# Values projected with the tokens standing, in a two-layer hybrid retention kernel

## The chip, the cores and the metric

The kernel runs as one program on one core of a Trainium2 chip. The metric is the device time of one execution in microseconds (us). Inputs lie in the chip's memory when it starts, and the output is written there.

## The reference, cut to what matters

A backbone of two layers over 512 latent tokens and 256 context tokens of width 1024, in float32. Each layer has a modulated RMS norm, one input projection whose columns feed three token mixers, an output projection, a second norm and a gated MLP with a convolution over tokens.

```python
q = _heads(p[..., Q0:K0], B, T)                          # p = h @ w_in, 512 columns each for q, k, v
k = _heads(p[..., K0:V0], B, T) * RET_HEAD_DIM ** -0.5
v = _heads(p[..., V0:G0], B, T)
q, k = apply_rope(q, cos, sin), apply_rope(k, cos, sin)  # latent tokens only
scores = jnp.einsum('bnihd,bnjhd->bnhij', qc, kc) * intra
o_intra = jnp.einsum('bnhij,bnjhe->bnihe', scores, vc)   # vc: values by chunk of 128 tokens
u = jnp.einsum('bnjhd,hj,bnjhe->bnhde', kc, zeta, vc)    # chunk states
o_cross = jnp.einsum('bnihd,hi,nbhde->bnihe', qc, xi, prev)
```

Keys, values and queries have 8 heads of 64. Both sums over j run over tokens, so TensorE wants values, and the keys of the states, with tokens on the partitions. Modulation vectors for later norms (`mods`) are dot products of columns of `w_mod` with silu(c).

## The kernel before, in words

**Layout.** Activations stand with features on the 128 partitions and tokens along the row: `h_hi`, `h_lo` are [128, 8 blocks, 768 tokens], the latent tokens first (0 to 511), then the context (512 to 767). Every number is split into a high part in the matmul's format and a rest, and each product is three matmuls: w_hi x_hi, w_lo x_hi, w_hi x_lo.

**Slabs.** All weights come as one stream of 206 slabs of 128 x 1024 numbers (512 KB), in the order of `stream_plan`. SP loads slab s into `raw[s % 2]` once slab s-2 is split (its wait on `split`); GpSimd splits each half into `w_hi[s % 2]` and `w_lo[s % 2]` (`split_half`, L475 and L477) once TensorE has finished the same half of slab s-2; TensorE multiplies (`tile`, L1316: one row block, three products, each over the column ranges `cols`) into the PSUM buffer `pair[s % 2]`, and ScalarE or VectorE copies it out and counts in `drained[s % 2]`. TensorE's `begin` waits for the first half's split and for the copy of slab s-2.

**The projection before.** Slabs 0 to 7 of a layer alternate one key block (128 features) and one value block, all 768 tokens; slabs 8 to 11 are the query blocks (layer 1: latent tokens only). Slabs 0 and 1 are interleaved with the norm that feeds them. ScalarE copies keys to `kT` and values to `Y` with features on the partitions. After each key and query slab, `swap` sends four DMAs from ScalarE's queue that copy the block with its 32-row quarters exchanged into `rot`, and VectorE's `rope` (L1007 to L1009) combines the two. During query slab 1 (the second), TensorE also transposes the values: after each of the first six row blocks, four 128x128 transposes for one chunk of 128 tokens (L1578) into one of two PSUM banks, which ScalarE copies to `vtok` (L674). During query slab 3 it does the same for the keys, into `ktok` (L680).

**Other work in this stretch.** ScalarE, in program order of layer 0 (L657 to L682): copy key 0, swap, copy value 0, Silu of `c_b` (L665), copy key 1, swap, copy value 1, wait for VectorE's L814 and Exp (L668), copy key 2, swap, copy value 2, the decay tables (`decays`, 28 small Exps, L515 to L526), copy key 3, swap, copy value 3, and then the value chunks and the queries. In layer 1 `decays` stands after value 0. VectorE, in order of layer 0: for each key j, rope and then `ring_mods` of 3, 3, 2, 2 modulation columns (`MODS_KVQ`; a column is two dot products over 1024, L790, and an addition, L793, which counts `mod_used`); after key 1's columns comes `log_decays` (L813 to L825), whose second instruction, L814, frees ScalarE's Exp. The dot products also write a scratch of 1024 columns in PSUM (`aux01`). The columns come through two slots: SP issues a slot's load only when `mod_used` shows it free, in one queue with the slab loads, so that here a slab's load stands behind a wait for VectorE (L392 to L403).

**After the projection**, the first mixer slabs (`mixer_plan`) run between the steps of retention, which VectorE paces with the masks and scaled values (`vz` from `vtok`, `St`, `qxi`).

```python
                act.wait_ge(s["decay_ready"], 1)
                for c in range(NLC + NCC):
                    act.wait_ge(s["tr_done"], c + 1)
                    nc.scalar.activation(vtok[:, c, :], aux(2 + c % 2), ACT.Copy).then_inc(s["v_moved"], 1)
```

Of the kernel before, what the change touches and what calls it, by code (L numbers as in the profile page):

```python
# [18 lines left out]
P = 128  # L19
T, C = 512, 256  # L20
# [36 lines left out]
def stream_plan():  # L57

    at, plan = 0, {}
    for l in range(DEPTH):  # L60
        for name, n in (("kv", 2 * HB), ("q", HB), ("cch", 2 * FB), ("cbf", 2 * FB), ("g", HB),
                        ("dft", dft_slabs(l)), ("out", KB)):
            plan[l, name] = at
            at += n
        for g, n in enumerate(GROUPS):
            plan[l, "up", g] = at
            at += 2 * n
            plan[l, "down", g] = at
            at += KB
    plan["end"] = at  # L70
    return plan


PLAN = stream_plan()


# [44 lines left out]
MODS_OUT = 2  # L121
MODS_UP = 2
MIXER_LEAD = KB
MIXER_TAIL = 4
# [53 lines left out]
def build_program(nc, io):  # L178
# [6 lines left out]
    def at(name, shape, offset, dt=fp32):  # L185
        return nc.alloc_sbuf_tensor_at(name, shape, dt, offset=offset)
# [46 lines left out]
    vtok = at("vtok", [P, NLC + NCC, 4 * P], work + 49152)  # L233
    z = at("z", [P, FB, TC], work + 61440)
    state = at("state", [P, NLC + 1, H, HD], work + 67584)
    St = at("St", [P, 2, 4, CH], work + 79872)
# [109 lines left out]
    with block:  # L346

        @block.sync
        def _(sp):
# [67 lines left out]
            for g, n in enumerate(GROUPS):  # L417
# [21 lines left out]
            s = PLAN[1, "kv"]  # L439
            load_slabs(s, 1)  # L440
# [15 lines left out]
        def _(pool):  # L456
# [30 lines left out]

            behind = {PLAN[0, "up", 0] + 2: "n2_0", PLAN[1, "kv"] + 2: "n1_1", PLAN[1, "up", 0] + 2: "n2_1"}
            for s in range(PLAN["end"]):
# [6 lines left out]
        def _(act):  # L496
# [135 lines left out]
            for l in range(DEPTH):  # L632
# [23 lines left out]

                kv, q0 = PLAN[l, "kv"], PLAN[l, "q"]  # L657
                for j in range(HB):
                    copy_out(kv + 2 * j, kT[:, j, :], TC)
                    swap(kT[:, j, 0:T], kv + 2 * j, j)  # L660
                    copy_out(kv + 2 * j + 1, Y[:, j, :], TC)
                    if j == 0:
                        if l == 0:
                            act.wait_ge(c_loaded, 32)
                            nc.scalar.activation(c_b[:, :, :], c_b[:, :, :], ACT.Silu).then_inc(c_ready, 1)  # L665
                    if l == 0 and j == 1:
                        act.wait_ge(ld_ready, 1)
                        nc.scalar.activation(ldt[:, 0, :], ldt[:, 1, :], ACT.Exp, scale=-1.0).then_inc(ld_ready, 1)  # L668
                    if j == (0 if l else 2):
                        decays(l)  # L670
                act.wait_ge(s["decay_ready"], 1)
                for c in range(NLC + NCC):
                    act.wait_ge(s["tr_done"], c + 1)
                    nc.scalar.activation(vtok[:, c, :], aux(2 + c % 2), ACT.Copy).then_inc(s["v_moved"], 1)  # L674
                for j in range(HB):
                    if j == HB - 1:
                        for c in range(NLC + NCC):
                            u = NLC + NCC + c
                            act.wait_ge(s["tr_done"], u + 1)
                            nc.scalar.activation(ktok[:, c, :], aux(2 + u % 2), ACT.Copy).then_inc(s["k_moved"], 1)  # L680
                    copy_out(q0 + j, Y[:, j, 0:nlat], nlat)
                    swap(Y[:, j, 0:T], q0 + j, HB + j)  # L682

                def gate(j):
# [93 lines left out]
        def _(dve):  # L778
# [7 lines left out]

            def mod_dots(slab, col, acc, used):

                for st in range(2):
                    chain(nc.vector.tensor_tensor_reduce(out=aux01[:, :], in0=slab, in1=c_b[:, st, :], scale=1.0,  # L790
                                                         scalar=0.0, op0=ALU.mult, op1=ALU.add,
                                                         accum_out=mod_acc[:, acc, st:st + 1]), mod_dots.base)
# [5 lines left out]
            def ring_mods(m, n):  # L798
                for j in range(m, m + n):
                    dve.wait_ge(mod_loaded[j % 2], 16 * (j // 2 + 1))  # L800
                    mod_dots(mod_slot[j % 2][:, :], MOD_START + j, j % 2, mod_used)

# [193 lines left out]
            for l in range(DEPTH):  # L996
# [14 lines left out]
                for j in range(HB):  # L1011
                    if j == 0:
                        dve.wait_ge(consts_loaded, 16 * 4)
                    rope(kT[:, j, 0:T], j)
                    if l == 0:
                        if j == 0:
                            dve.wait_ge(c_ready, 2)
                        ring_mods(m, MODS_KVQ[j])
                        m += MODS_KVQ[j]
                    elif j < 2:  # L1020
                        ring_mods(m, MODS_LAST)
                        m += MODS_LAST

                    if l == 0 and j == 1:
                        log_decays()
                    if j == (0 if l else 2):
                        decays(l)
                    if l and j == 1:
                        dve.wait_ge(mod_used, m)
                for j in range(HB):  # L1030
                    if l == 0 and j % 2:
                        ring_mods(m, MODS_KVQ[HB + j // 2])
# [275 lines left out]
        def _(pe):  # L1308
# [207 lines left out]
            for l in range(DEPTH):  # L1516
# [16 lines left out]
                def parts_ready(hi_sem, lo_sem, per):  # L1533

                    return lambda n: ((hi_sem, per * (n + 1)), (lo_sem, per * (n + 1)))

                kv_rest = (all_k, h_hi, h_lo, both, parts_ready(n1["hi_ready"], n1["h_ready"], 2))
                if l == 0:
# [14 lines left out]
                else:  # L1553
                    pair_behind_norm(PLAN[l, "kv"], "n1_1")
                slabs(PLAN[l, "kv"] + 2, HB - 1, all_k, h_hi, h_lo, both, None)

                n = 0
                for j in range(HB):
                    q = PLAN[l, "q"] + j
                    if j == 1:  # L1560
                        pe.wait_ge(*drained_by(PLAN[l, "kv"] + 2 * HB - 1))
                        pe.wait_ge(n1["nt_ready"], 2 * KB)
                    elif j == 3:
                        pe.wait_ge(s["roped"], HB)
                    begin(j % 2, q, pair_uses(q - j % 2))
                    for k in range(KB):
                        tile(j % 2, q, k, all_k, h_hi, h_lo, cols, None)
                        if j % 2 == 0 or k >= NLC + NCC:
                            continue
                        if n >= 2:  # L1570
                            last = n - 2
                            if last < NLC + NCC:
                                pe.wait_ge(s["v_moved"], last + 1)
                            else:
                                pe.wait_ge(s["k_moved"], last - (NLC + NCC) + 1)
                        src = Y if j == 1 else kT
                        for b in range(HB):
                            ins = nc.tensor.transpose(aux(2 + n % 2)[:, b * P:b * P + P], src[:, b, k * CH:k * CH + CH],  # L1578
                                                      ident[:, :])
                        ins.then_inc(s["tr_done"], 1)  # L1580
                        n += 1


                n_state = n_chunk = 0
# [25 lines left out]
                for item in mixer_plan(l):  # L1610
# [242 lines left out]
```

## Time and profile before

| | us |
|---|---|
| three runs, median | 1607.3 |
| lowest, highest | 1603.33, 1608.1 |
| the profiled execution's own time | 1607.85 |
| its span | 1606.1 |

| engine | busy us | share of the span | instructions |
|---|---|---|---|
| TensorE, matmuls (PE) | 1547.5 | 96% | 8910 |
| TensorE, weight loads (PEld) | 1296.8 | 81% | 8910 |
| VectorE (DVE) | 933.3 | 58% | 1331 |
| ScalarE (ACT) | 340.9 | 21% | 529 |
| GpSimd (POOL) | 900.5 | 56% | 841 |

The mean granted clock of TensorE was 0.987 of full speed. Matmuls are pipelined: they overlap in the profile, so the distance between two starts tells what one costs in a stream, and its duration does not. Weight loads lie beside the matmuls. An idle time in brackets is that of the engine before the instruction, with what ended it. DMA issues stand under the queue of the engine that sends them (ACTq, SPq). Layer 0's input projection lies between about 26 and 147 us, layer 1's between about 960 and 1059 us.

### The profile page before, as it was taken

Reading aid. Unit: us, or ns where it says so; the run is one execution under the profiler, and the core shown is the slowest. Engines: PE = TensorE matmul, PEld = TensorE weight load, DVE = VectorE, ACT = ScalarE, POOL = GpSimd, SP = SyncE. Lnnn points to the kernel's source line nnn. Section 1 sums busy time; section 2 is a strip of 40 time slices with the busy share of each in tenths; the row PEclk is TensorE's granted clock in tenths of the full one; section 3 lists DMA queues with packets and bytes.
Section 4 is the critical chain, followed back from the end, with each engine's and each line's share of the span. In section 5 each row is a group of like instructions: output and inputs, shape, how many; then the busy total and the mean of one; then the engine's idle time right before and its main releaser. Section 6 shows DMA issues by size and latency. Waiting matters only on the chain.

```text
span 1606.1 us, 24230 instructions
## 1 busy us (share of the span) xinstructions
PE 1547.5 (96%) x8910; PEld 1296.8 (81%) x8910; DVE 933.3 (58%) x1331; ACT 340.9 (21%) x529; POOL 900.5 (56%) x841
## 2 busy tenths in 40 slices
PE   7999989999999999999999999998999999999997
PEld 5888778886888888888888878876777888888886
DVE  4695556697788847882488547366555441341434
ACT  4332112313211101120012224111323220220221
POOL 2364233656555645554555446563475777777773
PEclk9999999999999999999999999999999999999999
DMA  9344111343333333332333222231122322223222
GB/s 377 133 144 132 40 33 47 129 159 117 108 114 131 131 130 119 118 118 65 118 118 127 83 91 93 79 105 53 53 92 66 100 96 92 97 99 106 95 92 100
DMA packets 50080, 172.70 MB, mean 108 GB/s; under 512 B 6240, under 2 KB 8800, under 8 KB 48992
## 3 DMA queue, kind: packets, MB, share of 16 engines
q1 hardware_dynamic: 46080, 165.70, 30.5%
q10 hardware_dynamic: 3936, 6.14, 1.3%
q8 instruction: 41, 0.67, 0.2%
q14 instruction: 23, 0.19, 0.0%
HBM read 165.52 MB, written 2.10 MB: 104 GB/s over the span
## 4 chain that ended last, share of the span: by engine, by line
PE 84%; DVE 9%; DMA 2%; POOL 2%; ACT 1%; issue 1%; SPq 0%; ACTq 0%; DVEq 0%; POOLq 0%
PE pair L1316 76%; PE pair L1425 3%; DVE qxi L1130 2%; DVE h_lo L939 1%; DVE nt L933 1%; DMA start_slot<-in_start_mods 1%; POOL w_lo L477 1%; PE aux L1662 1%; DMA raw<-in_slabs 1%; PE aux L1668 1%; PE aux L1578 1%; PE aux L1626 1%; DVE St L1134 1%; DVE aux L790 1%; POOL w_hi L475 1%
## 5 line engine op out<-in xcount | busy, mean ns | idle before, releaser
L475 POOL TENSOR_SCALAR w_hi<-raw 128x512 fp32r<-128x512 f32 (+1 forms) x410 | 300.4, 733 | 634.6 <-PE pair L1316 523.1
L477 POOL TENSOR_TENSOR w_lo<-raw,w_hi 128x512 fp32r<-128x512 f32 (+1 forms) x410 | 585.5, 1428 | 34.3
L1316 PE MATMUL pair<-h_hi,w_hi 128*128 128x512 f32 x1760 | 531.2, 360 | 6.8 <-DVE tv L1254 2.2
L1316 PE MATMUL pair<-h_lo,w_hi 128*128 128x512 f32 x1760 | 527.2, 357 | 2.7 <-DVE h_lo L1156 2.6
L1316 PE MATMUL pair<-h_hi,w_lo 128*128 128x512 f32 x1760 | 523.9, 355 | 0.0
L1316 PEld LDWEIGHTS pair<-h_hi,w_hi 128*128 128x128 f32 x1760 | 289.2, 189 | 64.6 <-issue 6.9
L1316 PEld LDWEIGHTS pair<-h_lo,w_hi 128*128 128x128 f32 x1760 | 289.3, 189 | 53.5 <-DVE h_lo L1156 4.2
L1316 PEld LDWEIGHTS pair<-h_hi,w_lo 128*128 128x128 f32 x1760 | 287.7, 189 | 47.5
L790 DVE CUSTOM_DVE_ANT_0 aux<-mod_slot,c_b 128x1024 f32<-128x1024 f32 x160 | 223.9, 1399 | 4.3 <-DMA mod_slot<-in_mods 1.1
L1209 DVE SCALAR_TENSOR_TENSOR x<-pair,modv,x 128x256 f32 (+3 forms) x84 | 53.0, 658 | 173.2 <-PE pair L1316 173.0
L1316 PE MATMUL pair<-hid_lo,w_hi 128*128 128x512 f32 x486 | 147.7, 358 | 0.0
L1316 PE MATMUL pair<-hid_hi,w_hi 128*128 128x512 f32 x486 | 147.3, 357 | 0.0
L1316 PE MATMUL pair<-hid_hi,w_lo 128*128 128x512 f32 x486 | 146.5, 356 | 0.0
L1254 DVE SCALAR_TENSOR_TENSOR tg<-pair,vecs,tg 128x511 f32<-128x511 f32 (+1 forms) x132 | 87.1, 660 | 84.9 <-ACT tg L763 76.8
L1254 DVE SCALAR_TENSOR_TENSOR tv<-pair,vecs,tv 128x511 f32<-128x511 f32 (+1 forms) x132 | 87.2, 661 | 81.2 <-ACT tv L760 73.0
L1316 PEld LDWEIGHTS pair<-hid_hi,w_hi 128*128 128x128 f32 x486 | 80.2, 188 | 14.8
L1316 PEld LDWEIGHTS pair<-hid_hi,w_lo 128*128 128x128 f32 x486 | 80.0, 187 | 14.8
L760 ACT ACTIVATE tv<-pair,vecs 128x768 f32<-128x768 f32 (+1 forms) x44 | 35.0, 796 | 266.4 <-PE pair L1316 208.6
L1316 PEld LDWEIGHTS pair<-hid_lo,w_hi 128*128 128x128 f32 x486 | 80.6, 188 | 13.6
L763 ACT ACTIVATE tg<-pair,vecs 128x768 f32<-128x768 f32 (+1 forms) x44 | 35.0, 795 | 193.1 <-PE pair L1316 190.3
L1282 DVE TENSOR_TENSOR hid_lo<-tv,hid_hi 128x768 f32 (+1 forms) x44 | 47.1, 1070 | 44.7 <-ACT hid_hi L768 44.7
L1425 PE MATMUL pair<-h_lo,w_hi 128*128 128x256 f32 (+1 forms) x160 | 53.6, 335 | 7.8 <-DVE h_lo L939 6.1
(171 smaller groups left out, 1294.7 us busy)
## 6 DMA issues: line engine op xcount, KB each, us to landing
raw<-in_slabs SPq DMA_DIRECT2D x206, 512.0 KB, 3.5
mod_slot<-in_mods SPq DMA_DIRECT2D x80, 512.0 KB, 3.5
start_slot<-in_start_mods SPq DMA_DIRECT2D x8, 1024.0 KB, 15.6
x<-in_x SPq DMA_DIRECT2D x4, 768.0 KB, 10.1
rot<-kT ACTq DMA_DIRECT2D x32, 64.0 KB, 3.3
rot<-Y ACTq DMA_DIRECT2D x32, 64.0 KB, 2.1
out<-fin SPq DMA_DIRECT2D x16, 128.0 KB, 1.9
c_b<-in_c SPq DMA_DIRECT2D x1, 512.0 KB, 7.6
```

Of the source, the lines that this page charges most:

```text
L475: nc.gpsimd.tensor_scalar(w_hi[p][:, a:b], raw[p][:, a:b], 1.0, 1.0, ALU.mult, ALU.mult).then_inc(split, 1)
L477: nc.gpsimd.tensor_tensor(w_lo[p][:, a:b], raw[p][:, a:b], w_hi[p][:, a:b].bitcast(fp32), ALU.subtract).then_inc(split, 3 if narrow(s) else 1)
L760: nc.scalar.activation(tv[:, 0:nlat], pair[0][:, 0:nlat], ACT.Copy, scale=vec_dyn("ffnw", w))\
L763: nc.scalar.activation(tg[:, 0:nlat], pair[1][:, 0:nlat], ACT.Copy, scale=vec_dyn("ffnw", w + 3 * NHB)).then_inc(s["tg_ready"], 1)
L790: chain(nc.vector.tensor_tensor_reduce(out=aux01[:, :], in0=slab, in1=c_b[:, st, :], scale=1.0, scalar=0.0, op0=ALU.mult, op1=ALU.add, acc ...
L933: nc.vector.scalar_tensor_tensor(nt[k % 2][:, a:b], aux(2 + part)[:, 0:b - a], mod(l, st, sc, k), x[:, k, a:b], ALU.mult, ALU.mult).then_i ...
L1130: nc.vector.tensor_tensor(qxi[to, hh, :, :], q[r], xi[r, d, :, :], ALU.mult)\
L1209: nc.vector.scalar_tensor_tensor(x[:, 2 * i + p, a0:a1], pair[p][:, a0:a1], modv[:, st, bass.ds(2 * i + (c0 + p), 1)], x[:, 2 * i + p, a0: ...
L1254: ins = nc.vector.scalar_tensor_tensor(dst, src, vec_dyn("ffnw", w + tap), dst, ALU.mult, ALU.add)
L1282: nc.vector.tensor_tensor(hid_lo[:, i, 0:nlat], tv[:, 0:nlat], hid_hi[:, i, 0:nlat].bitcast(fp32), ALU.subtract)\
L1316: ins = nc.tensor.matmul(out[:, a:b], wt, xt[:, a:b], start=first and k == 0, stop=last and k == 2)
L1425: ins = nc.tensor.matmul(pair[p][:, a:b], wt[p][:, w], xt[:, k, a:b], start=opens and j == 0, stop=n == len(order) - 1 and j == 2, skip_gr ...
```

## The change

Values are computed with the tokens on the partitions at once: the stationary operand is a 128x128 tile of `h_hi` or `h_lo`, the moving one 512 value columns of the weights. A value slab now holds two feature blocks (k = 2j and 2j+1) of all 512 value columns. TensorE runs, for each of the two blocks and each of six token chunks, three matmuls of 512 columns, and all four value slabs accumulate in six PSUM banks: the two of `pair[1]` and the four of `aux`. After the last, ScalarE copies the six banks to `vtok`. The transposes of values and the copies of values to `Y` are gone.

The twelve slabs come in a new order: keys in 0, 1, 2, 4, values in 3, 5, 7, 9, queries in 6, 8, 10, 11. Keys are transposed in the last two query slabs: four chunks in the second half of slab 10, two at the start of slab 11, and the banks go around all four of `aux`. ScalarE's two early steps stand after key slab 1 (Silu of `c_b`, then the wait for L814 and Exp), and in layer 1 `decays` stands there too. The scratch of the dot products in this stretch is `spare`, in SBUF. VectorE's first `vz` waits for the value copies, and TensorE's wait on `mod_used` before the first scores goes.

```diff
-        for name, n in (("kv", 2 * HB), ("q", HB), ("cch", 2 * FB), ("cbf", 2 * FB), ("g", HB),
+        for name, n in (("kvq", 3 * HB), ("cch", 2 * FB), ("cbf", 2 * FB), ("g", HB),
...
+K_SLABS, V_SLABS, Q_SLABS = [0, 1, 2, 4], [3, 5, 7, 9], [6, 8, 10, 11]
+def k_slab(l, j):
+    return PLAN[l, "kvq"] + K_SLABS[j]
...
+KEYS_EARLY = 4
...
+    spare = at("spare", [P, D], work + 12288)
...
+    def v_bank(c):
+        return pair[1][:, c * 4 * P:(c + 1) * 4 * P] if c < 2 else aux(c - 2)
+    V_ORDER = [0, 1, 4, 5, 2, 3]
+    def key_bank(c):
+        return aux((c + 2) % 4)
...
+                def move_values():
+                    act.wait_ge(s["decay_ready"], 1)
+                    act.wait_ge(done, v_slab(l, HB - 1) + 1)
+                    for n, c in enumerate(V_ORDER):
+                        ins = nc.scalar.activation(vtok[:, c, :], v_bank(c), ACT.Copy)
+                        if n == 1:
+                            ins.then_inc(drained[1], HB)
+                        else:
+                            ins.then_inc(s["v_moved"], 1)
+                def move_keys(first, last):
+                    for c in range(first, last):
+                        act.wait_ge(s["tr_done"], c + 1)
+                        nc.scalar.activation(ktok[:, c, :], key_bank(c), ACT.Copy).then_inc(s["k_moved"], 1)
...
                 for j in range(HB):
-                    copy_out(kv + 2 * j, kT[:, j, :], TC)
-                    swap(kT[:, j, 0:T], kv + 2 * j, j)
-                    copy_out(kv + 2 * j + 1, Y[:, j, :], TC)
-                    if j == 0:
-                        if l == 0:
-                            act.wait_ge(c_loaded, 32)
-                            nc.scalar.activation(c_b[:, :, :], c_b[:, :, :], ACT.Silu).then_inc(c_ready, 1)
+                    copy_out(k_slab(l, j), kT[:, j, :], TC)
+                    swap(kT[:, j, 0:T], k_slab(l, j), j)
                     if l == 0 and j == 1:
+                        act.wait_ge(c_loaded, 32)
+                        nc.scalar.activation(c_b[:, :, :], c_b[:, :, :], ACT.Silu).then_inc(c_ready, 1)
                         act.wait_ge(ld_ready, 1)
                         nc.scalar.activation(ldt[:, 0, :], ldt[:, 1, :], ACT.Exp, scale=-1.0).then_inc(ld_ready, 1)
-                    if j == (0 if l else 2):
+                    if j == (1 if l else 2):
                         decays(l)
...
                 for j in range(HB):
-                    if j == HB - 1:
...
+                    if j == 2:
+                        move_values()
+                        move_keys(0, KEYS_EARLY)
+                    elif j == 3:
+                        move_keys(KEYS_EARLY, NLC + NCC)
+                    copy_out(q_slab(l, j), Y[:, j, 0:nlat], nlat)
+                    swap(Y[:, j, 0:T], q_slab(l, j), HB + j)
...
-                        ring_mods(m, MODS_KVQ[j])
+                        ring_mods(m, MODS_KVQ[j], spare)
...
+                dve.wait_ge(s["v_moved"], NLC + NCC - 1)
                 scaled_values(0)
...
+                def values(j):
+                    slab_ = v_slab(l, j)
+                    pe.wait_ge(split, 4 * slab_ + 2)
+                    if j == 0:
+                        pe.wait_ge(*drained_by(k_slab(l, 1)))
                         pe.wait_ge(n1["nt_ready"], 2 * KB)
+                    for half in range(2):
+                        if half:
+                            pe.wait_ge(split, 4 * slab_ + 4)
+                        k, w = 2 * j + half, slice(half * 4 * P, (half + 1) * 4 * P)
+                        for c in range(NLC + NCC):
+                            t = slice(c * P, c * P + P)
+                            for n, (xt, wt) in enumerate(((h_hi, w_hi), (h_hi, w_lo), (h_lo, w_hi))):
+                                ins = nc.tensor.matmul(v_bank(c), xt[:, k, t], wt[1][:, w], start=k == 0 and n == 0,
+                                                       stop=k == KB - 1 and n == 2)
+                        ins.then_inc(done if half else half_done[1], 1)
+                def turn_keys(c):
+                    if c < 4:
+                        pe.wait_ge(s["v_moved"], c + 2)
+                    else:
+                        pe.wait_ge(s["k_moved"], c - 3)
...
+                for n in range(2, 3 * HB):
+                    if n in V_SLABS:
+                        values(V_SLABS.index(n))
+                        continue
+                    p, sl = n % 2, k0 + n
+                    uses = both if n in K_SLABS else cols
+                    begin(p, sl, pair_uses(sl - p))
+                    if n == Q_SLABS[2]:
                         pe.wait_ge(s["roped"], HB)
...
+                        if n == Q_SLABS[2] and k >= KB - KEYS_EARLY:
+                            turn_keys(k - (KB - KEYS_EARLY))
+                        elif n == Q_SLABS[3] and k < NLC + NCC - KEYS_EARLY:
+                            turn_keys(KEYS_EARLY + k)
...
-                            if l == 0:
-                                pe.wait_ge(mod_used, sum(MODS_KVQ))
```

## Rows read from the trace of the kernel before

**Rows 1.** The page's chain that ended last, shares of the span by engine.
```profile
PE 84%; DVE 9%; DMA 2%; POOL 2%; ACT 1%; issue 1%; SPq 0%; ACTq 0%; DVEq 0%; POOLq 0%
```

**Rows 2.** Chain in order of time, layer 0's projection; start us, us, what.
```profile
50.78 66.34 PE pair L1316 x374
```

**Rows 3.** TensorE's timeline, layer 1; start us, us, instruction xcount [idle before <-releaser].
```profile
979.03 0.51 PE L1316 MATMUL pair<-h_hi,w_hi 128*128 128x512 f32 x2
...
1029.91 0.40 PE L1316 MATMUL pair<-h_hi,w_hi 128*128 128x512 f32 x1
...
1036.07 0.60 PE L1578 MATMUL aux<-ident_small,Y 128*128 128x128 f32 x4
...
1037.19 0.60 PE L1578 MATMUL aux<-ident_small,Y 128*128 128x128 f32 x4
...
1054.00 0.66 PE L1578 MATMUL aux<-ident_small,kT 128*128 128x128 f32 x4 [1.75 <-ACT ktok L680]
```

**Rows 4.** ScalarE's timeline, layer 0's projection.
```profile
58.12 0.81 ACT L645 ACTIVATE Y<-pair 128x768 f32<-128x768 f32 x1 [3.74 <-issue]
...
60.24 1.92 ACT L665 ACTIVATE c_b<-c_b 128x2048 f32<-128x2048 f32 x1
65.22 0.81 ACT L645 ACTIVATE kT<-pair 128x768 f32<-128x768 f32 x1 [3.06 <-PE pair L1316]
66.06 2.44 ACTq L655 DMA_DIRECT2D rot<-kT  x4
73.70 0.81 ACT L645 ACTIVATE Y<-pair 128x768 f32<-128x768 f32 x1 [7.67 <-PE pair L1316]
...
88.77 0.24 ACT L668 ACTIVATE ldt<-ldt 128x48 f32<-128x48 f32 x1 [12.96 <-DVE ldt L814]
88.92 0.79 ACT L645 ACTIVATE kT<-pair 128x768 f32<-128x768 f32 x1
...
105.43 0.81 ACT L645 ACTIVATE kT<-pair 128x768 f32<-128x768 f32 x1
```

**Rows 5.** Line L1578, TensorE's transposes: duration ns min/median/max, first and last start.
```profile
L1578 PE MATMUL aux<-ident_small,Y x48: 270/272/273, 117.0 to 1042.0; 128*128 128x128 f32 x48
```

**Rows 6.** VectorE's timeline, the same stretch.
```profile
64.84 0.16 DVE L793 TENSOR_TENSOR modv<-mod_acc,vecs 128x2 f32<-128x2 f32 x1
...
68.85 1.23 DVE L790 CUSTOM_DVE_ANT_0 aux<-mod_slot,c_b 128x1024 f32<-128x1024 f32 x1 [1.11 <-DMA mod_slot<-in_mods]
...
73.00 0.80 DVE L1007 TENSOR_TENSOR rot<-rot,rope_sin 128x512 f32<-128x512 f32 x1 [1.12 <-DMA rot<-kT]
...
76.44 1.22 DVE L790 CUSTOM_DVE_ANT_0 aux<-mod_slot,c_b 128x1024 f32<-128x1024 f32 x1
...
88.03 0.18 DVE L813 TENSOR_SCALAR ldt<-vecs 128x48 f32<-128x48 f32 x1
```

**Rows 7.** SP's timeline, the same stretch: DMA issues.
```profile
65.03 0.33 SPq L365 DMA_DIRECT2D mod_slot<-in_mods  x1
65.40 0.43 SPq L351 DMA_DIRECT2D raw<-in_slabs  x1
```

**Rows 8.** GpSimd's timeline, the same stretch.
```profile
71.96 1.29 POOL L477 TENSOR_TENSOR w_lo<-raw,w_hi 128x512 fp32r<-128x512 f32 x1
```

**Rows 9.** Windows in retention: us; PE, PEld, DVE, ACT, POOL busy (x); PEclk; DMA; GB/s.
```profile
174.00:177.00 3.00, 0.52 (x7) 0.55 (x9) 2.27 (x4) 0.00 (x0) 0.00 (x0) 0.95 0.00 0
177.00:180.00 3.00, 3.00 (x29) 2.46 (x25) 0.00 (x0) 0.00 (x0) 0.00 (x0) 0.50 0.00 0
...
183.00:186.00 3.00, 3.00 (x22) 2.27 (x21) 0.00 (x0) 1.93 (x2) 1.81 (x2) 0.92 0.00 0
```

**Rows 10.** ScalarE's timeline, layer 1, its decays.
```profile
982.27 1.28 ACT L515 ACT_TABLE_LOAD   x1
...
991.00 0.42 ACT L526 ACTIVATE cdec<-ld 64x8 f32<-64x8 f32 x2
```

**Rows 11.** Waits of TensorE; us in total, times, longest us.
```profile
PE aux L1662 <- DVE St L1134: 17.2, 7, 6.2
```

More of the change, by code:

```diff
@@ L74, with v_slab, q_slab @@
 PLAN = stream_plan()
+K_SLABS, V_SLABS, Q_SLABS = [0, 1, 2, 4], [3, 5, 7, 9], [6, 8, 10, 11]
+def k_slab(l, j):
+    return PLAN[l, "kvq"] + K_SLABS[j]
+def v_slab(l, j):
+    return PLAN[l, "kvq"] + V_SLABS[j]
+def q_slab(l, j):
+    return PLAN[l, "kvq"] + Q_SLABS[j]
 def slab_blocks(s):
@@ L438, in _ @@
                     load_slabs(PLAN[0, "down", g] + 2 + 2 * i, 1)
-            s = PLAN[1, "kv"]
+            s = PLAN[1, "kvq"]
             load_slabs(s, 1)
@@ L486, in lows @@
                         .then_inc(pool_low, 1)
-            behind = {PLAN[0, "up", 0] + 2: "n2_0", PLAN[1, "kv"] + 2: "n1_1", PLAN[1, "up", 0] + 2: "n2_1"}
+            behind = {PLAN[0, "up", 0] + 2: "n2_0", PLAN[1, "kvq"] + 2: "n1_1", PLAN[1, "up", 0] + 2: "n2_1"}
             for s in range(PLAN["end"]):
@@ L667, in _ @@
                         act.wait_ge(ld_ready, 1)
                         nc.scalar.activation(ldt[:, 0, :], ldt[:, 1, :], ACT.Exp, scale=-1.0).then_inc(ld_ready, 1)
-                    if j == (0 if l else 2):
+                    if j == (1 if l else 2):
                         decays(l)
[L671 to L674, printed above, removed]
@@ L675, in _ @@
                 for j in range(HB):
-                    if j == HB - 1:
[L677 to L682, printed above, removed]
+                    if j == 2:
[3 more added lines that the diff above has]
+                        move_keys(KEYS_EARLY, NLC + NCC)
@@ L785, in chain, with mod_dots @@
                 dve.wait_ge(dve_chain, steps[0] if base is None else base + steps[0])
-            def mod_dots(slab, col, acc, used):
+            def mod_dots(slab, col, acc, used, scratch=aux01):
                 for st in range(2):
-                    chain(nc.vector.tensor_tensor_reduce(out=aux01[:, :], in0=slab, in1=c_b[:, st, :], scale=1.0,
+                    chain(nc.vector.tensor_tensor_reduce(out=scratch[:, :], in0=slab, in1=c_b[:, st, :], scale=1.0,
                                                          scalar=0.0, op0=ALU.mult, op1=ALU.add,
@@ L796, in _, with ring_mods @@
             mod_dots.base = None
-            def ring_mods(m, n):
+            def ring_mods(m, n, scratch=aux01):
                 for j in range(m, m + n):
                     dve.wait_ge(mod_loaded[j % 2], 16 * (j // 2 + 1))
-                    mod_dots(mod_slot[j % 2][:, :], MOD_START + j, j % 2, mod_used)
+                    mod_dots(mod_slot[j % 2][:, :], MOD_START + j, j % 2, mod_used, scratch)
             def one_plus(l, kind, ready):
@@ L1017, in _ @@
                             dve.wait_ge(c_ready, 2)
-                        ring_mods(m, MODS_KVQ[j])
+                        ring_mods(m, MODS_KVQ[j], spare)
                         m += MODS_KVQ[j]
                     elif j < 2:
-                        ring_mods(m, MODS_LAST)
+                        ring_mods(m, MODS_LAST, spare)
                         m += MODS_LAST
@@ L1031, in _ @@
                     if l == 0 and j % 2:
-                        ring_mods(m, MODS_KVQ[HB + j // 2])
+                        ring_mods(m, MODS_KVQ[HB + j // 2], spare)
                         m += MODS_KVQ[HB + j // 2]
@@ L1535, in parts_ready @@
                     return lambda n: ((hi_sem, per * (n + 1)), (lo_sem, per * (n + 1)))
+                k0 = PLAN[l, "kvq"]
                 kv_rest = (all_k, h_hi, h_lo, both, parts_ready(n1["hi_ready"], n1["h_ready"], 2))
@@ L1553, in _ @@
                 else:
[L1554 to L1561, printed above, removed]
-                        pe.wait_ge(n1["nt_ready"], 2 * KB)
-                    elif j == 3:
+                    pair_behind_norm(k0, "n1_1")
@@ new lines, in turn_keys @@
+                def turn_keys(c):
[3 more added lines that the diff above has]
+                        pe.wait_ge(s["k_moved"], c - 3)
+                    for b in range(HB):
+                        ins = nc.tensor.transpose(key_bank(c)[:, b * P:b * P + P], kT[:, b, c * CH:c * CH + CH], ident[:, :])
+                    ins.then_inc(s["tr_done"], 1)
+                for n in range(2, 3 * HB):
[6 more added lines that the diff above has]
+                    if n == Q_SLABS[2]:
@@ L1564, in _ @@
                         pe.wait_ge(s["roped"], HB)
-                    begin(j % 2, q, pair_uses(q - j % 2))
                     for k in range(KB):
[L1567 to L1581, printed above, removed]
+                        tile(p, sl, k, all_k, h_hi, h_lo, uses, None)
@@ L1802 @@
         k0, v0, g0, f0, cb0, cc0, ch0 = 4, 8, 12, 16, 18, 20, 22
-        order = [b + j for j in range(HB) for b in (k0, v0)] + list(range(HB))
-        order += [b + j for j in range(FB) for b in (cc0, ch0)] + [b + j for j in range(FB) for b in (cb0, f0)]
+        kvq = np.empty((3 * HB,) + w.shape[1:], w.dtype)
+        kvq[K_SLABS], kvq[Q_SLABS] = w[k0:k0 + HB], w[:HB]
+        kvq[V_SLABS] = np.asarray(w_in)[l][:, v0 * P:(v0 + HB) * P].reshape(HB, 2, P, HB * P).transpose(0, 2, 1, 3)\
+            .reshape(HB, P, 2 * HB * P)
+        slabs.append(kvq)
+        order = [b + j for j in range(FB) for b in (cc0, ch0)] + [b + j for j in range(FB) for b in (cb0, f0)]
         slabs.append(w[order + list(range(g0, g0 + HB))])
```

1 line of the change is left out of this document (removed).

## The prediction

> **What bounds the kernel now.** I read the chain that ended last first. TensorE holds 84% of it, VectorE 9% [rows 1]: a step counts when it changes what TensorE executes or makes TensorE wait. In the chain piece by piece, layer 0's input projection is one unbroken TensorE stretch: 374 matmuls in 66.34 us [rows 2]. They come in sixes (a row block: three products, each 512 + 256 columns), so a block takes 66.34 / 374 x 6 = 1.064 us and a slab of 8 blocks 8.51 us. Next I read TensorE's timeline in layer 1: six key and value slabs from 979.03 to 1029.91, 8.48 us each; then, for queries, 512 columns only: 27 matmuls from 1029.91 to 1036.07, 0.228 us each [rows 3]. The duration of one matmul there (0.40 us) is not its price; the distance between starts is. Last I read what the other engines do beside it in layer 0, because the change reorders their queues. ScalarE's timeline has the row that decides: after the value copy at 73.70 it does nothing until 88.77, when VectorE's L814 lets the small Exp of L668 go; only then is the key slab that ended in between copied out (88.92) [rows 4].
>
> **Values on TensorE.** Before, a value slab is 48 matmuls of 24 x 768 = 18432 columns, 8.48 to 8.51 us. After, it is 6 token chunks x 3 products x 2 blocks = 36 matmuls of 512 columns, again 18432. Each has its own weight load, like the query matmuls, so 36 x 0.228 = 8.20 us [rows 3]. Saved: 0.3 us a slab, 1.2 us a layer. No row shows six banks taken in turn: the bounds are zero (0.008 us more a matmul) and twice the estimate, 0.6 us a slab.
>
> **Transposes of values.** 6 groups of 4 go in each layer. Two groups start 1.12 us apart with three matmuls between (0.68), so a group costs 0.44 us [rows 3]: 2.6 us a layer. One lasts 0.27 us [rows 5], but they overlap one another, and that is no price.
>
> The Trainium skill ("TensorE: Matmul & The Clock Gate", Part 4: PE-mode transpose) puts a 128x128 transpose at some 275 ns in a kernel. By that figure removing 24 would give 6.6 us a layer, 8 us more over both; an estimate from that page, and a rival below. The duration agrees with this trace, the distance between starts does not.
>
> **Keys' transposes and ScalarE.** Keys are still transposed, 6 groups. In layer 1 TensorE loses some 1.9 us at the third group (row 1054.00, 1.75 of it idle): ScalarE had to send three sets of DMAs first. After, the six value copies start when the last value slab ends, and the first group needs three of them. A copy of 768 columns takes 0.81 us [rows 4], so three of 512 take at most 2.4; the group is due after five row blocks of 0.68, 3.4 us on. That wait goes. ScalarE also loses four copies of 0.81 a layer, which lie beside TensorE and are worth nothing. Layer 1: 1.2 + 2.6 + 1.9 = 5.7 us saved.
>
> **The wait that is added, layer 0.** In the new ScalarE order the two instructions that were spread out now stand together, after key slab 1: Silu of c_b, then the wait for VectorE's L814, then Exp. Only behind them is the third key slab (slab 2) copied out of pair[0], and slab 4, the fourth key slab, now wants pair[0] two slabs earlier than the next use did. Before, what was queued behind that wait was slab 4's copy, there at 89.7 and needed by slab 6 at 73.3 + 2 x 8.51 = 90.3: hidden with 0.6 us to spare. Now it is slab 2's, needed when slab 3 ends. Step by step:
> - Slab 2 ends at 65.2 and slab 3 at 73.7 by the copies that follow them [rows 4]. The starts are 0.4 earlier; with the shorter value slab TensorE would begin slab 4 at 73.0 (before: 73.3).
> - c_b's Silu moves behind the second swap. Copy to 58.9, four DMA issues 2.44, table load 1.3 (58.9 to 60.2), Silu 1.92: ready at 64.6 instead of 62.2 [rows 4].
> - VectorE's first modulation column then ends at 67.4, not 65.0. The third needs a slot whose load SP issues on that signal and which takes 65.03 to 68.85 = 3.8 us: it runs 71.3 to 74.0 [rows 6, 7].
> - The rotated key is already there, so rope follows: 3.4 us (73.00 to 76.44), to 77.4. Three columns took 76.44 to 88.03, 11.6 us [rows 6]. That would be 89.0. Undisturbed, a column takes 2.8 (62.2 to 65.0, against 3.9 in the 11.6) and rope three operations of 0.8 (row 73.00); then the load of the last (issued when the fourth is used, 74.0 + 2.4 + 2.8 = 79.2, and 3.8 long) sets 83.0 + 2.8 = 85.8. GpSimd will run out of slabs to split on the way, since TensorE stands still, so I take 87.5, between the two.
> - From L813 to the end of slab 2's copy: 88.03 to 89.7 before, so 1.7 us [rows 4, 6]. TensorE begins slab 4 at 89.2, bounds 87.5 to 90.7. It waits 16.2 us and is 15.9 us later than before.
>
> Slab 4's weights would have been late too: their load is issued behind the same modulation signal (65.40), and its first half was split at 71.96 + 1.29 = 73.25, just when wanted [rows 7, 8]; 2.4 us later makes 75.7. That 2.7 us lies inside the wait and counts only if the wait isn't there.
>
> **What follows in layer 0.** The fourth key slab can be copied only when ScalarE's decays are done, at 105.43 [rows 4], and query slab 6 needs that buffer; at 89.2 + 2 slabs = 105.9 this costs 0.5 us or, with a slow clock, nothing. VectorE's ropes and later columns keep their times; they had waited for TensorE. The three value slabs left save 0.9, the transposes 2.6.
>
> **The clock.** In the trace, TensorE's granted clock is at 0.95 in the 3 us in which it stands waiting, then 0.50 (1.2 of 2.4 GHz) for the next 3, and back to 0.92 by 183 to 186 [rows 9]. Seven microseconds at half rate are up to 3.5 us lost after a gap of some 3 us. After 16 us idle I take 2.0 us, between 0 and 3.5.
>
> The Trainium skill ("TensorE: Matmul & The Clock Gate", "Why this matters for your kernels") says that a matmul burst after an idle gap starts at half clock. The trace agrees; by it the added wait has a second price and none of it comes back, which is how I count.
>
> Layer 0: 15.9 + 2.0 - 0.9 - 2.6 = +14.4 us (the 0.5 lies under the 2.0).
>
> **Layer 1 has no such wait.** There ScalarE's decays move from behind the first key slab to behind the second. They take 982.27 to 991.4, 9.2 us [rows 10]. After: second copy and DMAs to 984.8, decays to 994.0, slab 2's copy to 994.8. Slab 4 wants the buffer at 979.0 + 8.5 + 8.2 = 995.7: hidden by 0.9 us. If that cover were short by 1 us it would cost 1 us.
>
> The other edits cost nothing: VectorE's dot products write to SBUF instead of PSUM, 12 columns in layer 0 and 4 in layer 1, beside TensorE. If they were 10% quicker or slower, the long wait would move by 0.8 us either way. The dropped wait on mod_used is passed long before.
>
> **Sum.** The profiled execution took 1607.85 us, 0.5 over the median of the three shown. 1607.85 + 14.4 - 5.7 = 1616.6; against the median 1616.
>
> **Rivals.**
> A. The other side: ScalarE's wait doesn't reach TensorE, because VectorE passes L814 before slab 3 ends. It decides from the point where slab 4 begins by 89.2 - 8.8 = 80.4, that is L814 done by 78.7. For it: the second key is slab 1 now, so its rotated copy never keeps VectorE waiting. Against: three columns must still be loaded and computed after 74.0, at 2.8 us each without any delay 82.4. With the wait gone, the late weights of slab 4 alone remain: +2.7 and some 0.5 for the clock, less 1.2 + 2.6 in layer 0 and 5.7 in layer 1: 1601.5.
> B. The gains are larger than start distances say: each of 48 transposes worth its whole duration, 0.27 us, so 13.0 instead of 5.2. 1616.6 - 7.8 = 1608.8, no change. Against it: the distances of [rows 3]. (This is where the Trainium skill's figure of 275 ns leads.)
> C. A wait in retention takes the gain of layer 1. TensorE already waits there for VectorE's St, 17.2 us in 7 times [rows 11]. If VectorE's chain there were tied to a transfer and not to TensorE, up to 5.7 us would come back as waiting: 1622. Against: its chain there starts from ropes and states, and both follow TensorE's slabs. With the highest bounds of the wait and the clock beside it (+1.5, +1.5): 1625.
>
> **Chances.** Forecast 0.76, A 0.08, B 0.05, C 0.11. A change under 0.3% (4.8 us) can't be told from none. The forecast's own range comes from the wait (-1.7, +1.5), the clock (-2, +1.5), the gains (+-2): 1611 to 1621, and C and a little of B widen it to 1610 to 1623. Faster is A: 0.08. Within 0.3%: B and the low tail of the forecast, 0.08. Slower: 0.84.
>
> **What would show it.** In the changed profile: TensorE idle some 16 us from about 73, released by ScalarE's kT copy; ScalarE idle before its small Exp until VectorE's L814; half clock in the slice after; value matmuls 0.228 us apart; no ktok wait in layer 1 and its projection 5.7 us shorter. I am wrong if slab 4 begins before 80, if TensorE's value slabs take over 8.5 us, or if layer 1 has a wait for the third key copy.

## The result, and the profile after

The changed kernel takes 1615.61 us (median of 5 runs, 1614.51 to 1617.76) against 1607.3 (median of 5, 1603.33 to 1608.1): ratio 1.0059, 95% interval 1.0046 to 1.0073, so slower by 7 to 12 us. The prediction was 1616.0. The profiled execution after took 1615.61, its span is 1613.8.

The page of the changed kernel, busy time of TensorE (144 matmuls fewer) and the chain by engine, which answers to [rows 1]: TensorE has 3 points less of the chain and VectorE 3 more.

```profile
PE 1539.8 (95%) x8766; PEld 1289.0 (80%) x8766; DVE 935.0 (58%) x1331; ACT 333.3 (21%) x521; POOL 902.3 (56%) x841
...
PE 81%; DVE 12%; DMA 3%; ACT 2%; POOL 2%; issue 1%; ACTq 0%; SPq 0%; DVEq 0%; POOLq 0%
```

TensorE's waits in the changed kernel between 40 and 160 us, its layer 0 projection (us in total, times, longest); before there was none in that stretch.

```profile
PE pair L1352 <- ACT kT L673: 16.8, 1, 16.8
```

ScalarE's timeline of the changed kernel in layer 0, to be laid beside [rows 4]. The idle in brackets before the small Exp is 23.25 us, not 12.96, and the copy of slab 2 (91.03, now the third key) stands right behind. Before, the copy of slab 2 (then the second key) began at 65.22 with nothing in front of it.

```profile
55.35 0.82 ACT L673 ACTIVATE kT<-pair 128x768 f32<-128x768 f32 x1 [3.12 <-PE pair L1352]
...
59.55 0.82 ACT L673 ACTIVATE kT<-pair 128x768 f32<-128x768 f32 x1 [3.38 <-issue]
...
63.12 1.28 ACT L706 ACT_TABLE_LOAD   x1 [2.75 <-issue]
64.41 1.92 ACT L706 ACTIVATE c_b<-c_b 128x2048 f32<-128x2048 f32 x1
...
90.88 0.24 ACT L708 ACTIVATE ldt<-ldt 128x48 f32<-128x48 f32 x1 [23.25 <-DVE ldt L849]
91.03 0.79 ACT L673 ACTIVATE kT<-pair 128x768 f32<-128x768 f32 x1
...
103.01 0.81 ACT L673 ACTIVATE kT<-pair 128x768 f32<-128x768 f32 x1
```

Between 66 and 91 us VectorE decides, as in [rows 6]. Its timeline in the changed kernel: the third modulation column waits for its load, then come the second key's rope and three more columns, and at 90.43 the table steps that free ScalarE.

```profile
68.97 1.22 DVE L825 CUSTOM_DVE_ANT_0 spare<-mod_slot,c_b 128x1024 f32<-128x1024 f32 x1
...
72.94 1.23 DVE L825 CUSTOM_DVE_ANT_0 spare<-mod_slot,c_b 128x1024 f32<-128x1024 f32 x1 [1.28 <-DMA mod_slot<-in_mods]
...
75.84 0.68 DVE L1042 TENSOR_TENSOR rot<-rot,rope_sin 128x512 f32<-128x512 f32 x1
...
79.13 2.28 DVE L825 CUSTOM_DVE_ANT_0 spare<-mod_slot,c_b 128x1024 f32<-128x1024 f32 x1
...
90.43 0.18 DVE L848 TENSOR_SCALAR ldt<-vecs 128x48 f32<-128x48 f32 x1
90.64 0.21 DVE L849 TENSOR_TENSOR ldt<-ldt,vecs 128x48 f32<-128x48 f32 x1
```

The chain in order of time of the changed kernel, layer 0 (start us, us, what). The fourth key slab takes 11.00 us instead of 8.5; a value slab is a line of pair and a line of aux for each of its halves, 1.37 + 2.72 + 1.36 + 2.72 = 8.17 us; the next query slab has 8.47.

```profile
91.97 11.00 PE pair L1352 x48
102.97 1.38 PE pair L1607 x6
104.35 2.72 PE aux L1607 x12
107.08 1.36 PE pair L1607 x6
108.44 2.72 PE aux L1607 x12
111.16 8.47 PE pair L1352 x48
```

The granted clock in the wait and behind it, in windows of the changed kernel (us; PE, PEld, DVE, ACT, POOL busy; PEclk; DMA; GB/s): the clock falls to half while TensorE stands still (0.65 is the mean of 14 us of the wait, and the slice from 82 to 85 alone has 0.50), and is back some 5 us after it starts again at 91.97.

```profile
76.00:90.00 14.00, 0.00 (x0) 0.00 (x0) 13.76 (x16) 0.00 (x0) 11.13 (x7) 0.65 0.52 166
...
82.00:85.00 3.00, 0.00 (x0) 0.00 (x0) 2.97 (x4) 0.00 (x0) 3.00 (x2) 0.50 0.00 0
...
93.00:96.00 3.00, 3.00 (x11) 2.52 (x11) 1.84 (x10) 0.96 (x4) 0.00 (x0) 0.50 0.50 149
96.00:99.00 3.00, 3.00 (x16) 2.59 (x16) 2.93 (x4) 3.00 (x12) 0.03 (x1) 0.79 0.00 0
99.00:102.00 3.00, 3.00 (x20) 2.61 (x19) 2.93 (x6) 3.00 (x12) 2.73 (x2) 1.00 0.02 5
```

Where the 7.7 us between the two spans lie follows from four starts in each kernel: the copy of the first key slab and of the last query slab, in either layer. After these are 55.35 above and the three rows that follow; before they are 53.56, 146.66, 977.08 and 1059.48.

```profile
163.99 0.81 ACT L673 ACTIVATE Y<-pair 128x768 f32<-128x768 f32 x1 [4.43 <-PE pair L1352]
...
991.17 0.81 ACT L673 ACTIVATE kT<-pair 128x768 f32<-128x768 f32 x1 [1.81 <-PE pair L1461]
...
1067.44 0.61 ACT L673 ACTIVATE Y<-pair 128x512 f32<-128x512 f32 x1 [1.69 <-PE pair L1352]
```

| stretch | before | after | difference |
|---|---|---|---|
| start to layer 0's first key copy | 53.56 | 55.35 | +1.79 |
| layer 0's projection, to the last query copy | 93.10 | 108.64 | +15.54 |
| from there to layer 1's first key copy | 830.42 | 827.18 | -3.24 |
| layer 1's projection | 82.40 | 76.27 | -6.13 |
| from there to the end of the span | 546.62 | 546.36 | -0.26 |

Two of the five are not touched by the edits and still move: the start, and the stretch between the projections. In the six kernels below the first copy lies between 53.2 and 55.0 and the second stretch takes 828.3 to 831.3. They vary by some 2 to 3 us, opposite to each other here.

For the start the traces say what it is: the same code ran under another granted clock. The two windows below are those of the kernel before (0.95) and of the changed one (0.86). In the slice from 30 to 35 us the clock was 1.00 before, 0.50 in the changed kernel. Over all eight traces the first copy lies at 53.2 to 53.6 where that slice had 1.00 (before, e1, e2, e4), at 53.9 and 54.3 where it had 0.88 and 0.93 (e5, e6), at 55.0 and 55.4 where it had 0.50 (e3, changed).

```profile
26.00:60.00 34.00, 31.58 (x217) 23.27 (x217) 17.70 (x41) 12.13 (x23) 7.84 (x9) 0.95 0.61 229
```

```profile
26.00:60.00 34.00, 32.11 (x206) 22.96 (x207) 17.10 (x40) 10.53 (x22) 6.37 (x8) 0.86 0.60 227
```

In the stretch between the projections the changed kernel has some 3.4 us less of half clock than the kernel before (summed over windows of 3 us). That is worth 1.7 us at most; the rest of the 3.2 us was not settled. TensorE's waits there are alike, 20.7 us before and 22.5 after.

In layer 1 TensorE's timeline of the changed kernel shows the groups of key transposes 1.12 to 1.13 us apart (1057.04, 1058.16, 1059.29) with no wait among them; [rows 3] had 1.75 us of idle at the third group, here at 1059.29:

```profile
1057.04 0.60 PE L1617 MATMUL aux<-ident_small,kT 128*128 128x128 f32 x4
...
1059.29 0.60 PE L1617 MATMUL aux<-ident_small,kT 128*128 128x128 f32 x4
```

### The profile page after: what moved, and what is told of

It reads as the page before. It is cut to its first block, busy times and chain, and to the rows that moved or that the text cites. A ratio compares the mean times of both kernels' runs of the same rounds, so it can differ in the third digit from the quotient of the medians.

```text
span 1613.8 us, 23888 instructions
## 1 busy us (share of the span) xinstructions
PE 1539.8 (95%) x8766; PEld 1289.0 (80%) x8766; DVE 935.0 (58%) x1331; ACT 333.3 (21%) x521; POOL 902.3 (56%) x841
## 4 chain that ended last, share of the span: by engine, by line
PE 81%; DVE 12%; DMA 3%; ACT 2%; POOL 2%; issue 1%; ACTq 0%; SPq 0%; DVEq 0%; POOLq 0%
PE pair L1352 70%; PE pair L1461 3%; PE aux L1607 2%; DVE qxi L1166 2%; DVE h_lo L974 1%; PE pair L1607 1%; DVE nt L968 1%; DMA start_slot<-in_start_mods 1%; DVE vz L1104 1%; DMA raw<-in_slabs 1%; DVE spare L825 1%; POOL w_lo L505 1%; PE aux L1713 1%; DVE state L1112 1%; PE aux L1719 1%
## 5 line engine op out<-in xcount | busy, mean ns | idle before, releaser
L1352 PE MATMUL pair<-h_hi,w_hi 128*128 128x512 f32 x1632 | 497.3, 361 | 23.3 <-ACT kT L673 16.8
L1352 PE MATMUL pair<-h_lo,w_hi 128*128 128x512 f32 x1632 | 492.9, 358 | 3.5 <-DVE h_lo L1192 3.3
L1352 PE MATMUL pair<-h_hi,w_lo 128*128 128x512 f32 x1632 | 489.7, 356 | 0.0
L1352 PEld LDWEIGHTS pair<-h_hi,w_hi 128*128 128x128 f32 x1632 | 270.0, 190 | 77.4 <-issue 23.6
L1352 PEld LDWEIGHTS pair<-h_lo,w_hi 128*128 128x128 f32 x1632 | 269.1, 189 | 50.9 <-DVE h_lo L1192 5.5
L1352 PEld LDWEIGHTS pair<-h_hi,w_lo 128*128 128x128 f32 x1632 | 268.3, 189 | 44.3
L825 DVE CUSTOM_DVE_ANT_0 aux<-mod_slot,c_b 128x1024 f32<-128x1024 f32 x128 | 175.0, 1367 | 2.3
## 6 DMA issues: line engine op xcount, KB each, us to landing
start_slot<-in_start_mods SPq DMA_DIRECT2D x8, 1024.0 KB, 15.5
```

The source lines that it names most:

```text
L825: chain(nc.vector.tensor_tensor_reduce(out=scratch[:, :], in0=slab, in1=c_b[:, st, :], scale=1.0, scalar=0.0, op0=ALU.mult, op1=ALU.add, a ...
L1352: ins = nc.tensor.matmul(out[:, a:b], wt, xt[:, a:b], start=first and k == 0, stop=last and k == 2)
```

## The experiments

Theory 1 is the prediction's: ScalarE holds the copy of the third key slab behind a wait for VectorE's L849 (L814 before), and TensorE waits for that copy. Its rival is that VectorE or the loads limit this stretch whichever order ScalarE has. All times below are medians; the kernel before took 1607.45 us beside the first four experiments and 1607.8 beside the last two.

### e1: the wait, the Exp and the decay tables behind the fourth key

```diff
                         nc.scalar.activation(c_b[:, :, :], c_b[:, :, :], ACT.Silu).then_inc(c_ready, 1)
+                    if l == 0 and j == 3:
                         act.wait_ge(ld_ready, 1)
                         nc.scalar.activation(ldt[:, 0, :], ldt[:, 1, :], ACT.Exp, scale=-1.0).then_inc(ld_ready, 1)
-                    if j == (1 if l else 2):
+                    if j == (1 if l else 3):
                         decays(l)
```

> The changed kernel with one thing moved in ScalarE's program of layer 0: the wait for VectorE's small table step (L849), the Exp behind it and the decay tables stand behind the fourth key's copy and DMAs, no longer behind the second key's and the third's. Silu of c_b stays behind the second key. Theory 1 (what stood still in TensorE was the copy of slab 2 queued behind ScalarE's wait): the 16.8 us wait goes, slab 4 begins when the late first half of its weights is split, some 2.6 us after slab 3's end (about 77.7 in the changed kernel's time), TensorE is hardly slowed by the clock: 14.3 us of wait and some 2 us of half clock come back, about 1599.5 us (1598 to 1602). Rival (VectorE's columns are the limit of this stretch, whichever order ScalarE has: the wait comes back at a later slab, at the third or fourth query): 1610 to 1616 us.

Measured: 1601.64 us, ratio to before 0.9963 (0.9948 to 0.9977); 14 us less than the changed kernel. TensorE's only wait in the stretch is the 2.6 us for the late weights. In e1's chain slab 4 takes 10.29 us:

```profile
74.03 1.66 POOL w_lo L505
...
75.73 10.29 PE pair L1353 x48
```

TensorE's waits in e1, the same stretch:

```profile
PE pair L1353 <- POOL w_lo L505: 2.6, 1, 2.6
```

The granted clock behind that wait, in a window of e1:

```profile
76.00:79.00 3.00, 3.00 (x14) 2.53 (x14) 2.96 (x3) 0.00 (x0) 2.53 (x3) 0.72 0.63 249
```

Theory 1 holds, the rival falls. The time lies 2 us above the expectation, and some 1.3 of them are the clock: behind the wait of 2.6 us the slab is still 1.8 us slower than 8.5, so that only 0.7 us of half clock came back and not 2. (e5 will show a wait of the same kind without that price.)

### e2: Silu of c_b in its old place as well

```diff
-                    if l == 0 and j == 1:
+                    if l == 0 and j == 0:
                         act.wait_ge(c_loaded, 32)
                         nc.scalar.activation(c_b[:, :, :], c_b[:, :, :], ACT.Silu).then_inc(c_ready, 1)
```

> As the previous kernel, and Silu of c_b stands again behind the first key's DMAs, ahead of the second key's copy. Theory 1: VectorE's first modulation column is some 3 us earlier again, with it the load of slab 4, so that TensorE has no wait at slab 4 either: 2.6 us of wait and a little half clock less than the previous kernel, about 1597 us. Rival (slab 4's weights were never late, only the copy was): the same time as the previous kernel, within 1 us.

Measured: 1598.03 us (1597.82 to 1600.33), ratio to before 0.9949 (0.9933 to 0.9966). This beats both kernels: 9.4 us less than before, 17.6 less than the changed kernel. Layer 0's projection takes 89.29 us, 3.8 less than before: with the wait gone, that is what the prediction gave four value slabs and the transposes of values (1.2 + 2.6). In e2's chain TensorE goes through slab 4 with 8.62 us and waits for nothing in the whole projection; the first half of slab 4's weights is split at 70.97 + 1.67 = 72.64, 0.2 us before it starts.

```profile
72.81 8.62 PE pair L1353 x48
```

GpSimd's timeline of e2:

```profile
70.97 1.67 POOL L505 TENSOR_TENSOR w_lo<-raw,w_hi 128x512 fp32r<-128x512 f32 x1
```

### e3: keys turned twice

```diff
-                    for b in range(HB):
+                    for b in list(range(HB)) * 2:
                         ins = nc.tensor.transpose(key_bank(c)[:, b * P:b * P + P], kT[:, b, c * CH:c * CH + CH], ident[:, :])
```

> As the previous kernel (e2), and TensorE turns each chunk of keys twice into the same bank, which gives the same result: 48 more transposes of 128x128 over both layers, the number that the change took away. If a transpose is worth the distance between starts (0.44 us for four with what they do to the next matmul, 0.35 without): 4.2 to 5.3 us more than the previous kernel. If it is worth its duration (0.27 us each): 13 us more.

Measured: 1601.44 us, 3.4 us above e2 and so below the expected 4.2 to 5.3; ratios to before 0.9968 (0.9958 to 0.9979) and 0.9949 (0.9933 to 0.9966), which overlap. The two traces say it more sharply: layer 0's projection takes 91.89 us against 89.29 and layer 1's 78.92 against 76.26, together 5.3 us. TensorE's timeline of e3: groups of eight with three matmuls between start 1.57 us apart, four more cost 0.45 us.

```profile
1041.81 1.03 PE L1618 MATMUL aux<-ident_small,kT 128*128 128x128 f32 x8
...
1043.38 1.03 PE L1618 MATMUL aux<-ident_small,kT 128*128 128x128 f32 x8
```

13 us are excluded. The duration of a transpose is not its price in a stream; the distance is.

### e4: TensorE kept busy in the wait

The added matmuls put products into value chunk 2 that don't belong there.

```diff
+                    if l == 0 and n == K_SLABS[3]:
+                        for _ in range(74):
+                            nc.tensor.matmul(v_bank(2), h_hi[:, 0, 0:P], h_hi[:, 1, 0:4 * P], start=False, stop=False)
```

> The changed kernel, with 74 more matmuls of 512 columns in layer 0 ahead of slab 4's wait, where TensorE stood still: they add products into the bank of value chunk 2 that don't belong there, so that the values of that chunk are wrong. They take 74 x 0.228 = 16.9 us, the length of the wait, and TensorE still waits for the same copy at the same time. Theory 1 with a price for the clock: slab 4 then runs at full clock, 8.5 us instead of 11.0, and the kernel takes 2.5 us less, about 1613 us. Rival (the clock price is not there or is paid elsewhere): 1615.6 us, no difference.

Measured: 1612.74 us, ratio to before 1.0039 (1.0026 to 1.0052) against 1.0059 (1.0046 to 1.0073) for the changed kernel: 2.9 us less. ScalarE's copy still ends the wait, of which 0.2 us are left (the first key copy of e4 lies 2 us earlier, at 53.37), and slab 4 takes 8.72 us where it took 11.00; the clock stays at 1.00:

```profile
89.05 0.80 ACT kT L673
...
89.99 8.72 PE pair L1352 x48
```

A window of e4 in what was the wait, and one behind it:

```profile
82.00:85.00 3.00, 3.00 (x15) 2.49 (x14) 2.93 (x6) 0.00 (x0) 2.92 (x3) 1.00 0.64 176
...
90.00:93.00 3.00, 3.00 (x17) 2.63 (x18) 2.56 (x13) 0.00 (x0) 0.00 (x0) 1.00 0.69 240
```

The half clock is a price of its own, on top of the wait. The intervals overlap, so the 2.9 us rest on the medians; the 2.3 us of slab 4 rest on the rows.

### e5: the wait behind the third key only

```diff
                         nc.scalar.activation(c_b[:, :, :], c_b[:, :, :], ACT.Silu).then_inc(c_ready, 1)
+                    if l == 0 and j == 2:
                         act.wait_ge(ld_ready, 1)
                         nc.scalar.activation(ldt[:, 0, :], ldt[:, 1, :], ACT.Exp, scale=-1.0).then_inc(ld_ready, 1)
```

> The changed kernel with only the wait and the Exp behind it moved, from behind the second key's DMAs to behind the third's; the decay tables stay behind the third, ahead of the fourth key's copy. Theory 1 (it is each time the copy queued behind VectorE's step that TensorE waits for): no wait at slab 4 but for its late weights (2.6 us), and a new one at slab 6, the next user of pair[0], until the fourth key is copied behind the tables at about 101 to 104: some 9 us of it, with half clock behind. About 1609 us (1607 to 1611), between the changed kernel and e1. Rival (any order that frees slab 2's copy is enough): the time of e1, 1601.6 us.

Measured: 1618.05 us, ratio 1.0057 (1.0041 to 1.0073): as slow as the changed kernel, and 9 us above the expectation, outside its range. The rival (1601.6) is out. The mechanism is the one expected, its size is not. TensorE waits 2.9 us at slab 4 and 15.2 us at slab 6:

```profile
PE pair L1353 <- ACT kT L673: 15.2, 1, 15.2
PE pair L1353 <- POOL w_lo L505: 2.9, 1, 2.9
```

The expectation had the tables done at 101 to 104; they end at 107.7. Two things made them late. First, the table steps began 1.9 us later than in the changed kernel, each counted from its first key copy; for 1.05 us of these VectorE stood waiting for the load of its third column behind the second key. Second, the table steps from L849 to L861 now take 90.88 to 99.75 = 8.9 us, where the same steps took 90.43 to 94.95 = 4.5 us in the changed kernel. What differs beside them is GpSimd: with TensorE going on, it splits slabs (in the windows of e5 it is busy 2.83 of the 3 us from 94 to 97), while in the changed kernel it had nothing to split from 87.9 to 98.97 (the last row below).

The half clock is paid once here, not twice. Slab 6, behind the long wait, takes 10.70 us. Slab 4, behind the wait of 2.9 us, starts at 76.60, the value slab after it at 85.19, 8.6 us later, and the clock stays at 1.00 (TensorE's timeline and two windows of e5):

```profile
76.60 0.62 PE L1353 MATMUL pair<-h_hi,w_hi 128*128 128x512 f32 x2 [2.91 <-POOL w_lo L505]
...
85.19 0.40 PE L1608 MATMUL pair<-w_hi,h_hi 128*128 128x512 f32 x1
```

```profile
76.00:79.00 3.00, 2.40 (x13) 2.12 (x14) 2.96 (x3) 0.00 (x0) 2.92 (x3) 1.00 0.87 328
79.00:82.00 3.00, 3.00 (x18) 2.58 (x18) 2.93 (x5) 0.00 (x0) 2.44 (x3) 1.00 0.01 5
```

Rows of e5: ScalarE's timeline, the chain at slab 6, and the window on GpSimd (the last of the five busy times).

```profile
92.42 0.25 ACT L709 ACTIVATE ldt<-ldt 128x48 f32<-128x48 f32 x1 [22.26 <-DVE ldt L850]
99.85 2.45 ACT L543 ACTIVATE mask<-expo,ld 128x128 f32<-128x128 f32 x8 [7.18 <-DVE ld L861]
...
107.73 0.81 ACT L673 ACTIVATE kT<-pair 128x768 f32<-128x768 f32 x1
```

```profile
108.68 10.70 PE pair L1353 x48
```

```profile
94.00:97.00 3.00, 0.00 (x0) 0.00 (x0) 2.83 (x6) 0.00 (x0) 2.83 (x5) 0.84 0.51 167
```

GpSimd's timeline of the changed kernel:

```profile
98.97 0.62 POOL L503 TENSOR_SCALAR w_hi<-raw 128x512 fp32r<-128x512 f32 x1 [11.08 <-PE pair L1352]
```

### e6: VectorE's table steps ahead of the columns

```diff
+                        if j == 1:
+                            log_decays()
                         ring_mods(m, MODS_KVQ[j], spare)
...
-                    if l == 0 and j == 1:
-                        log_decays()
```

> The changed kernel's ScalarE order is kept, and VectorE does its table steps (L848 on) before the second key's three modulation columns and not behind them. Theory 1 (the length of TensorE's wait is VectorE's time until its second table step): the three columns took some 11.4 us, so slab 4 begins 11 us earlier; a wait of 5 to 6 us is left, with nearly the same half clock: about 1604.5 us (1603 to 1607). Rival (ScalarE's wait is bound by something else, such as the table load or the DMAs of the swaps): 1613 us or more.

Measured: 1606.07 us, ratio 0.9988 (0.9978 to 0.9998); 9.5 us less than the changed kernel, within the expected range. The wait shrinks from 16.8 to 6.7 us and slab 4 still takes 10.74:

```profile
PE pair L1352 <- ACT kT L673: 6.7, 1, 6.7
```

The chain of e6:

```profile
80.59 10.74 PE pair L1352 x48
```

## Why the prediction was right

- **The added wait.** Predicted 16.2 us, bounds to 17.7; measured 16.8. e1 and e2 take it away by moving ScalarE's wait behind the copies of the keys, e6 shortens it by shortening what VectorE does first, e5 moves it to the next user of the buffer. That is the mechanism, shown from four sides. The stations, less the 1.79 us by which everything starts later: Silu done at 64.5 (predicted 64.6), third column from 71.2 (71.3), rope over at 77.4 (77.4), columns over at 88.6 (87.5), slab 4 from 90.2 (89.2). The station that was off is the three columns, 11.3 us against 10.1. Where GpSimd was splitting (until 87.9) a column took 3.8 us and more, the last one, with GpSimd idle, 2.6: I let GpSimd fall idle earlier than it did.
- **Late weights.** The 2.7 us hidden inside the wait came out in e1 as 2.6 and were gone in e2.
- **The clock.** Predicted 2.0 us between 0 and 3.5; slab 4 took 2.5 more. Rival A's half microsecond after a short wait was neither of the two values seen: 1.8 in e1, 0.1 at most in e5.
- **Values.** 8.17 us a slab, predicted 8.20. Six banks in turn cost nothing.
- **Transposes.** e3's 0.45 us for four, predicted 0.44. Rival B is out.
- **Layer 1.** Predicted 5.7 us, measured 6.1. The cover of the third key's copy was 1.05 us (copied by 1008.90, slab 4 from 1009.95), predicted 0.9. Rival C is out: TensorE waits 17.1 us for St after, 17.2 before ([rows 11]).
- **Layer 0.** Predicted +14.4, measured +15.5: the columns, 1.2 us longer than I gave them, and the clock, 0.5 us dearer, less some tenths in the gains. The 0.5 us for the decay tables, which lay under the clock's term, did not come: the fourth key was copied at 103.01, and slab 6 wanted its buffer at 111.16.

Nothing but waits and clock separates these kernels in layer 0's projection, as a comparison with e2 shows, whose projection (89.29 us) has no wait (all in us):

| kernel | longer than e2's projection | TensorE's waits | slab behind the wait, over 8.5 |
|---|---|---|---|
| e1 | 4.4 | 2.6 | 1.8 |
| e6 | 8.8 | 6.7 | 2.2 |
| changed | 19.4 | 16.8 | 2.5 |
| e5 | 20.6 | 2.9 and 15.2 | 0.1 and 2.2 |

The sum came closer than its parts: layer 0 was 1.1 us worse, layer 1 0.4 better, and the start and the middle stretch, which I had at zero, gave +1.8 and -3.2. That these nearly cancel is luck, and so is the hit on the median to 0.4 us.

## What to carry to other kernels

When slabs or buffers are renumbered, list for every in-order engine what is queued behind each of its waits, and when the buffer's next user wants it: an instruction that was 0.6 us from being late is the place where a new order breaks. Moving one wait only to the next gap is no cure (e5); it had to stand behind the last copy of its kind (e1, e2). And a wait of TensorE can cost more than its length: four of the five waits for a slab in layer 0's projection (2.6, 6.7, 15.2 and 16.8 us) were followed by a slab that was 1.8 to 2.5 us slower, one (2.9 us) was not. Read the granted clock behind a short wait before you price it.

## What the runs showed of the hardware that I had not expected

- Where the half clock was paid, it hardly depended on the length of the wait: the slab behind it took 11.00 us after 16.8 us of waiting, 10.70 after 15.2, 10.74 after 6.7, 10.29 after 2.6, against 8.5. But the length did not decide whether it was paid: e1's 2.6 us were followed by it, e5's 2.9 us were not. These are single executions, one of each kernel.
- The granted clock goes with the spread between executions of one kernel. Of the 27 executions of the kernel before that stood beside e1 to e4 the fastest (1602.25 us) had a mean granted clock of 0.991, the slowest (1610.54) 0.984.
- VectorE's table steps on 48 columns took 4.5 us with GpSimd idle and 7.9 to 10.6 us with GpSimd splitting slabs beside them, the longer the larger GpSimd's busy share over the steps: 7.9 us at 65% (e6), 8.5 at 70% (e1), 8.9 at 81% (e5), 9.4 at 83% (before, 88.03 to 97.46), 10.6 at 86% and 87% (e2, e3). TensorE's activity is not the cause: in e4 it was busy 4.07 of the first 4.32 us of the steps, GpSimd idle, and they took 4.5 us. Nor is it how busy the DMA engines are: their share was 0.88 and 0.87 in the two fast cases and 0.25 to 0.61 in the others. An engine that is off the path lengthened a wait on it; no run changed GpSimd's work by itself.
- Writing the dot products' scratch to SBUF and not PSUM made a column 0.1 us shorter, with GpSimd idle both times (66.36 to 68.97, against 62.19 to 64.92).
